# Two attentions of a decoder trunk: normalising after the product with the values

## The chip, the cores and the metric

The kernel runs on one core of one Trainium2 chip. The metric is the device time of one execution in microseconds, as the median of three runs; one further execution was recorded by the hardware profiler, and all rows shown here are from it. TensorE does the matrix products (PE in the rows; its weight loads are PEld and run beside the products), VectorE is DVE, ScalarE is ACT, GpSimd is POOL, SyncE (SP) issues the DMAs.

## The reference, cut to what matters

One layer of a trunk over 1024 positions of width 1024. Three branches (a latent attention, a forgetting attention, a state-space layer) are fed from one projection, gated, projected and summed; a gated feed-forward part with a convolution follows. Both attentions have 4 heads and this form:

```python
for i in range(seq // 128):                      # 8 query tiles
    s = q[tile i] @ k[:tile i + 1].T * scale     # (+ forget bias in one of them)
    p = softmax(where(causal, s, -1e30))
    out[tile i] = p @ v[:tile i + 1]             # values are 64 wide
```

All products keep float32 accuracy: each operand is split into a high part (fp32r) and the rest (lo), and three, or with exact weights two, products are added.

## The kernel before

The program is a chain of stages, each a block of five engine programs written out by hand with semaphores, and a barrier of all engines between blocks. The stage of the forgetting attention (names `fox_`, operands 66 wide) ends at 353 us of the span, that of the latent attention (`mla_`, `mlaa_`, 96 wide) at 576 us. Both end in a loop of the same class `Attention`, the first from 217 us on: 32 steps s = 0..31, step s is head h = s // 8 and query tile i = s % 8, with (i+1) x 128 keys. In between TensorE is given products of another part, the gates' projection (`GateFill`, L540), in fixed portions per step (`ATT_FILL`, `ATT_AHEAD`), so that it has work while the other engines deal with the softmax; the fill's matrix products need none of the attention's results.

One step goes through the engines so:

- TensorE `score` (L692, mask added by L694): scores into PSUM banks 0 to 3, two steps ahead of their use.
- VectorE `maximum` (L849): the row maximum. ScalarE `exponent` (L791): exponentials into `p_buf[s % 2]` and, by the accumulator, their row sum.
- VectorE `norm`: reciprocal of the sum (L855) and the whole row of exponentials times it, in place (L857).
- TensorE `turn` (L673; for queries and keys of the next head L678): 128 x 128 transposes through the identity, up to four into one PSUM bank. Each such bankful is a "fill of a bank", numbered in the list `fills`; fill f uses bank 4 + f % 2.
- ScalarE `split_hi` (L781) and VectorE `split_lo` (L862) empty the bank into the high and low parts of `pt`. Fill f of TensorE waits until fill f - 2 is emptied: `pe.wait_ge(self.lo, f - 1)`, since they share a bank. The semaphore `lo` counts VectorE's part.
- TensorE `values` (L720), every second step: the values times the turned rows of two query tiles, into bank 6. Four tiles (a group g, 8 in all) fill that bank. One half of its partitions has the product with the high part of the values, the other with the low part.
- ScalarE `out_low` (L805) copies the one half to `osum`, VectorE `out_sum` (L868) adds the other; for odd heads `out_hi` (L811) and `out_lo` (L875) split the sum for the next stage.

VectorE's order in step s is: `norm(s)`, with i = 7 the maximum of s + 1, `split_lo` of the fills of step s - 1, the maximum of s + 2 (not with i = 6), `split_lo` of the query and key fills, then `out_sum` (s % 4 = 1) or `out_lo` (s % 4 = 2). Engines run their programs strictly in order. TensorE's order at i = 5, where two bank fills of exponentials, p(s, first) and p(s, last), stand apart: first, six fill products, last; then step i = 6 begins with four fill products (`ATT_AHEAD`), the keys' fill, and so on.

After the last step TensorE does `values`, then `EDGE` = 10 fill products that cover the tail of the other engines, and the block ends with the barrier.

Of the kernel before, what the change touches and what calls it, by code (L numbers as in the profile page):

```python
# [21 lines left out]
P = 128  # L22
# [602 lines left out]
class Attention:  # L625
# [6 lines left out]

    def __init__(self, m, tag, kd, q_of, k_of, vv, q_t, k_t, p_buf, pt, osum, branch, ready, fill):
        self.m, self.kd, self.q_of, self.k_of, self.vv, self.q_t, self.k_t = m, kd, q_of, k_of, vv, q_t, k_t
        self.p_buf, self.pt, self.osum, self.branch, self.ready, self.fill = p_buf, pt, osum, branch, ready, fill
        (self.scores, self.negmax, self.exped, self.recip, self.normed, self.turned, self.hi, self.lo, self.pv,
         self.o_low, self.o_sum, self.o_hi, self.o_lo) = (m.sem(f"{tag}_{n}") for n in (
             "scores", "negmax", "exp", "recip", "norm", "turned", "hi", "lo", "pv", "o_low", "o_sum", "o_hi", "o_lo"))  # L640
        self.nmax, self.rsum, self.rinv = m.stat[:, 0:2], m.stat[:, 2:4], m.stat[:, 4:6]
        self.S = [m.ps[:, 2 * i:2 * i + 2, :].rearrange("p b n -> p (b n)") for i in range(2)]

        fills = [(w, 0, half) for w in "qk" for half in range(2)]
        for s in range(ATT_STEPS):
            fills += self.turned_in(s)
            fills += [("p", s, a, min(4, s % TT + 1 - a)) for a in range(0, s % TT + 1, 4)]
        self.fills = fills
        self.upto = {f[:2]: n + 1 for n, f in enumerate(fills)}
        self.at = {f: n for n, f in enumerate(fills)}  # L650

# [13 lines left out]
    def turn(self, pe, f):  # L665
        nc, m, x = self.m.nc, self.m, self.fills[f]
        if f >= 2:
            pe.wait_ge(self.lo, f - 1)
        bank = m.ps[:, 4 + f % 2, :]
        if x[0] == "p":  # L670
            _, s, a, n = x
            for j in range(n):
                tr = nc.tensor.transpose(bank[:, j * P:(j + 1) * P], self.p_buf[s % 2][:, (a + j) * P:(a + j + 1) * P], m.ident[:])  # L673
        else:
            what, h, half = x
            src = self.q_of if what == "q" else self.k_of
            for j in range(4):
                tr = nc.tensor.transpose(bank[0:self.kd, j * P:(j + 1) * P], src(h, 4 * half + j), m.ident[:])  # L678
        tr.then_inc(self.turned, 1)
# [44 lines left out]
    def tensor(self, pe):  # L724
        self.ready(pe)
        for what, n in zip("qk", OPENING):
            for f in self.fills_of(what, 0):
                self.turn(pe, f)
            self.fill.tensor(pe, n)
        self.score(pe, 0)  # L730
        self.score(pe, 1)
        for s in range(ATT_STEPS):
            i = s % TT
            if i == 7 and s + 1 < ATT_STEPS:
                self.score(pe, s + 1)
            if s + 2 < ATT_STEPS and i != 6:
                self.score(pe, s + 2)
            self.fill.tensor(pe, ATT_AHEAD[i])
            for f in self.qk_fills(s):
                self.turn(pe, f)  # L740
            pe.wait_ge(self.normed, s + 1)
            *first, last = self.fills_of("p", s)
            for f in first:
                self.turn(pe, f)

            if first:
                self.fill.tensor(pe, ATT_FILL[i])
            self.turn(pe, last)
            if not first:
                self.fill.tensor(pe, ATT_FILL[i])  # L750
            if s >= 2 and s % 2 == 0:
                self.values(pe, s // 2 - 1)
        self.values(pe, ATT_STEPS // 2 - 1)
        self.fill.tensor(pe, EDGE)


# [50 lines left out]
    def out_hi(self, act, g):  # L807
        h, half, _, _ = self.out_rows(g)
        if h % 2:
            act.wait_ge(self.o_sum, g + 1)  # L810
            self.m.nc.scalar.activation(self.m.br_hi[:, 2 * self.branch + h // 2, half * BANK:(half + 1) * BANK], self.osum[half],  # L811
                                        ACT.Copy).then_inc(self.o_hi, 1)

    def scalar(self, act):
        for what in "qk":
            for f in self.fills_of(what, 0):
                self.split_hi(act, f)
        self.exponent(act, 0)
        for s in range(ATT_STEPS):
            i = s % TT  # L820
            if s + 1 < ATT_STEPS:
                self.exponent(act, s + 1)
            if s % 4 == 1 and s > 4:
                self.out_low(act, s // 4 - 1)
            if s % 4 == 2 and s > 4:
                self.out_hi(act, s // 4 - 1)
            self.fill.scalar(act, ATT_AHEAD[i])
            for f in self.qk_fills(s):
                self.split_hi(act, f)
            *first, last = self.fills_of("p", s)  # L830
            for f in first:
                self.split_hi(act, f)
            if first:
                self.fill.scalar(act, ATT_FILL[i])
                self.fill.copy_made(act)
            self.split_hi(act, last)
            if not first:
                self.fill.scalar(act, ATT_FILL[i])
        g = ATT_STEPS // 4 - 1
        self.out_low(act, g)  # L840
        self.out_hi(act, g)
# [6 lines left out]
            dve.wait_ge(self.exped, s - 1)  # L848
        self.m.nc.vector.tensor_reduce(self.nmax[:, b:b + 1], self.S[b][:, 0:keys], AX.X, ALU.max, negate=True).then_inc(self.negmax, 1)  # L849

    def norm(self, dve, s):
        keys, b = (s % TT + 1) * P, s % 2
        V = self.m.nc.vector
        dve.wait_ge(self.exped, s + 1)
        V.reciprocal(self.rinv[:, b:b + 1], self.rsum[:, b:b + 1]).then_inc(self.recip, 1)  # L855
        dve.wait_ge(self.recip, s + 1)
        V.tensor_scalar(self.p_buf[b][:, 0:keys], self.p_buf[b][:, 0:keys], self.rinv[:, b:b + 1], None, ALU.mult).then_inc(self.normed, 1)  # L857

    def split_lo(self, dve, f):
        (hi, lo), src = self.place(f)  # L860
        dve.wait_ge(self.hi, f + 1)
        self.m.nc.vector.tensor_tensor(lo, src, f32(hi), ALU.subtract).then_inc(self.lo, 1)  # L862

    def out_sum(self, dve, g):
        h, half, main, _ = self.out_rows(g)
# [11 lines left out]
    def vector(self, dve):  # L877
# [5 lines left out]
        for s in range(ATT_STEPS + 1):  # L883
            h, i = divmod(s, TT)
            last = h + 1 >= H
            if s < ATT_STEPS:
                self.norm(dve, s)
            if i == 7 and not last:
                self.maximum(dve, s + 1)
            if s:  # L890
                for f in self.fills_of("p", s - 1):
                    self.split_lo(dve, f)
            if s + 2 < ATT_STEPS and i != 6:
                self.maximum(dve, s + 2)
            if s < ATT_STEPS:
# [1 line left out]
                    self.split_lo(dve, f)  # L897
            if s % 4 == 1 and s > 4:
                self.out_sum(dve, s // 4 - 1)
            if s % 4 == 2 and s > 4:  # L900
                self.out_lo(dve, s // 4 - 1)
        g = ATT_STEPS // 4 - 1
        self.out_sum(dve, g)
        self.out_lo(dve, g)


# [1955 lines left out]
```

## Time and profile before

| | |
|---|---|
| median of 3 runs | 1511.03 us (1509.42 to 1513.41) |
| profiled execution, its own time | 1511.12 us |
| its span in the profile | 1509.1 us |
| TensorE busy (products) | 1451.5 us, 96% of the span |
| VectorE busy | 1002.0 us, 66% |
| ScalarE busy | 652.2 us, 43% |
| TensorE idle in the forgetting attention, 216 to 353.2 us | 7.6 us in 12 waits |
| granted clock of TensorE, mean | 0.994 |

How to read the rows further down: in a timeline row stand the start in us, the duration in us (of all that are merged, where x is over 1), the engine, the line, the operation, what is written <- what is read, the shapes and the count; in square brackets the idle time of that engine just before and what ended it. In a row of waits stand who waited for whom, the total in us, how many times, and the longest.

### The profile page before, as it was taken

Reading aid. Unit: us, or ns where it says so; the run is one execution under the profiler, and the core shown is the slowest. Engines: PE = TensorE matmul, PEld = TensorE weight load, DVE = VectorE, ACT = ScalarE, POOL = GpSimd, SP = SyncE. Lnnn points to the kernel's source line nnn. Section 1 sums busy time; section 2 is a strip of 40 time slices with the busy share of each in tenths; the row PEclk is TensorE's granted clock in tenths of the full one; section 3 lists DMA queues with packets and bytes.
Section 4 is the critical chain, followed back from the end, with each engine's and each line's share of the span. In section 5 each row is a group of like instructions: output and inputs, shape, how many; then the busy total and the mean of one; then the engine's idle time right before and its main releaser. Section 6 shows DMA issues by size and latency. Waiting matters only on the chain.

```text
span 1509.1 us, 19008 instructions
## 1 busy us (share of the span) xinstructions
PE 1451.5 (96%) x7138; PEld 1218.5 (81%) x7138; DVE 1002.0 (66%) x1378; ACT 652.2 (43%) x1054; POOL 124.4 (8%) x104
## 2 busy tenths in 40 slices
PE   7999999998989998998999999999999999999999
PEld 6999887776877776886778888888888888888887
DVE  5211356665676666774872778877777787679786
ACT  6230235554435553124551255555555555444332
POOL 1000131001420003110210000000000000000000
PEclk9999999999999999999999999999999999999999
DMA  7101131113031102224664213222222221892222
GB/s 257 61 0 74 45 108 39 37 31 138 29 86 45 36 28 75 82 70 159 212 231 143 84 50 99 89 84 84 83 81 81 81 81 43 303 387 92 84 78 77
DMA packets 129941, 148.93 MB, mean 99 GB/s; under 512 B 11002, under 2 KB 94893, under 8 KB 129581
## 3 DMA queue, kind: packets, MB, share of 16 engines
q1 hardware_dynamic: 129664, 147.67, 29.6%
q8 instruction: 56, 0.92, 0.2%
q14 instruction: 32, 0.26, 0.1%
q10 hardware_dynamic: 189, 0.08, 0.0%
HBM read 110.83 MB, written 36.31 MB: 98 GB/s over the span
## 4 chain that ended last, share of the span: by engine, by line
PE 48%; issue 2%; DVE 1%; POOL 1%; ACT 0%; DMA 0%; POOLq 0%; DVEq 0%; ACTq 0%; SPq 0%
PE ps L1868 28%; PE ps L2175 4%; PE ps L2176 4%; PE ps L2177 4%; PE ps L2750 2%; PE ps L2751 2%; PE ps L2752 2%; POOL split_arena L2253 1%; PE ps L2264 1%; PE ps L2782 0%; DVE plain_arena L2271 0%; DMA plain_arena<-in_w_branch 0%; DVE plain_arena L2548 0%; PE ps L2760 0%; DVE down_all L2146 0%
## 5 line engine op out<-in xcount | busy, mean ns | idle before, releaser
L1868 PE MATMUL ps<-split_arena 128*128 128x512 f32 x1320 | 306.8, 389 | 0.0
L540 PE MATMUL ps<-split_arena 128*128 128x512 f32 x1152 | 290.0, 401 | 6.9 <-POOL split_arena L586 3.5
L1868 PEld LDWEIGHTS ps<-split_arena 128*128 128x128 f32 x1320 | 247.5, 188 | 51.5 <-issue 0.3
L540 PEld LDWEIGHTS ps<-split_arena 128*128 128x128 f32 x1152 | 211.1, 190 | 49.3 <-issue 5.7
L2051 ACT ACTIVATE down_ops<-down_all 128x1024 fp32r<-128x1024 f32 x77 | 81.6, 1061 | 115.5 <-PE ps L2177 112.1
L1868 PE MATMUL ps<-up_b,split_arena 128*128 128x512 f32 x528 | 126.5, 389 | 0.0
L2070 DVE TENSOR_TENSOR down_ops<-down_all,down_ops 128x1024 fp32r<-128x1024 f32 x77 | 94.1, 1223 | 46.3 <-ACT down_ops L2051 46.1
L2175 PE MATMUL ps<-down_ops 128*128 128x512 f32 x308 | 119.9, 389 | 0.5 <-DVE down_ops L2070 0.5
L2177 PE MATMUL ps<-down_ops 128*128 128x512 f32 x308 | 119.8, 389 | 0.0
L2176 PE MATMUL ps<-down_ops 128*128 128x512 f32 x308 | 119.8, 389 | 0.0
L1868 PEld LDWEIGHTS ps<-up_b,split_arena 128*128 128x128 f32 x528 | 99.1, 188 | 20.5
L327 PE MATMUL ps<-split_arena 128*128 128x426 f32 (+1 forms) x256 | 92.7, 362 | 2.2 <-DVE split_arena L213 2.2
L328 PE MATMUL ps<-split_arena 128*128 128x426 f32 (+1 forms) x256 | 91.5, 358 | 0.0
L329 PE MATMUL ps<-split_arena 128*128 128x426 f32 (+1 forms) x256 | 91.3, 357 | 0.0
L586 POOL TENSOR_TENSOR split_arena<-plain_arena,split_arena 128x1024 fp32r<-128x1024 f32 x23 | 61.0, 2652 | 347.6 <-ACT split_arena L564 347.6
L849 DVE TENSOR_REDUCE stat<-ps 128x1 f32<-128x128 f32 (+3 forms) x64 | 48.3, 755 | 51.9 <-PE ps L694 51.9
L465 DVE COPY plain_arena<-ps 128x426 f32<-128x426 f32 (+6 forms) x28 | 10.3, 406 | 104.0 <-PE ps L329 104.0
L2264 PE MATMUL ps<-split_arena 128*128 128x512 f32 x288 | 69.8, 401 | 6.4 <-PEq L2278 3.0
L575 ACT ACTIVATE plain_arena<-ps 128x512 f32<-128x512 f32 x48 | 28.6, 596 | 106.2 <-PE ps L540 61.5
L1796 DVE TENSOR_TENSOR split_arena<-up_s,split_arena 128x512 fp32r<-128x512 f32 x88 | 60.4, 687 | 18.3 <-ACT split_arena L1741 18.2
L2264 PEld LDWEIGHTS ps<-split_arena 128*128 128x128 f32 x288 | 54.6, 192 | 21.4 <-issue 5.6
L2175 PEld LDWEIGHTS ps<-down_ops 128*128 128x128 f32 x308 | 57.8, 188 | 13.0 <-DVE down_ops L2070 0.9
(359 smaller groups left out, 2523.6 us busy)
## 6 DMA issues: line engine op xcount, KB each, us to landing
plain_arena<-in_w_in SPq DMA_DIRECT2D x24, 512.0 KB, 4.1
scr_gate<-plain_arena SPq DMA_DIRECT2D x48, 256.0 KB, 2.0
plain_arena<-scr_gate SPq DMA_DIRECT2D x24, 512.0 KB, 4.3
plain_arena<-in_w_up SPq DMA_DIRECT2D x22, 512.0 KB, 5.3
up_raw<-in_w_up SPq DMA_DIRECT2D x22, 512.0 KB, 4.7
scr_act<-plain_arena SPq DMA_DIRECT2D x22, 512.0 KB, 2.7
down_all<-scr_act SPq DMA_DIRECT2D x18, 512.0 KB, 9.4
down_all<-in_w_down SPq DMA_DIRECT2D x18, 512.0 KB, 9.9
```

Source lines behind the costliest of these rows:

```text
L327: nc.tensor.matmul(o, hi, wh, start=(k == 0), stop=False)
L328: nc.tensor.matmul(o, hi, wl, start=False, stop=False)
L329: mm = nc.tensor.matmul(o, lo, wh, start=False, stop=(k == KD - 1))
L540: mm = nc.tensor.matmul(m.ps[:, self.banks[half], :], w[:, k, :], src[:, k, h * BANK:(h + 1) * BANK], start=(j == 0), stop=(j == self.PER_ ...
L586: self.m.nc.gpsimd.tensor_tensor(self.w_lo[u % 2], self.raw, f32(self.w_hi[u % 2]), ALU.subtract).then_inc(self.lo, 1)
L1868: mm = nc.tensor.matmul(o, self.w[j][w][:, k, :], self.h[j][k][h], start=(j in self.OPENS and k == 0 and n == 0), stop=(k == self.HK - 1 a ...
L2051: self.m.nc.scalar.activation(self.hi_of[n % 3], self.pair(n)[0], ACT.Copy).then_inc(self.hi, 1)
L2070: self.m.nc.vector.tensor_tensor(self.lo_of[n % 3], self.pair(n)[0], f32(self.hi_of[n % 3]), ALU.subtract).then_inc(self.lo, 1)
L2175: nc.tensor.matmul(o, a_hi[:, cut], b_hi, start=(k == 0 and j in self.OPENS), stop=False, skip_group_check=True)
L2176: nc.tensor.matmul(o, a_hi[:, cut], b_lo, start=False, stop=False, skip_group_check=True)
L2177: mm = nc.tensor.matmul(o, a_lo[:, cut], b_hi, start=False, stop=(k == HF - 1), skip_group_check=True)
L2264: mm = nc.tensor.matmul(proj_ps[u % 2][:, cut], w[:, k, :], src[:, 2 * n + k, cut], start=(k == 0 and w is hi and src is m.br_hi), stop=(k ...
```

## The change

The exponentials are turned and multiplied with the values as they are. VectorE takes only the reciprocal of each row sum (kept for 8 steps, `rinv` has 8 columns now), and the multiplication of the rows (L857) is left out. Instead the sums of four query tiles are scaled together: after the values of group g TensorE turns four columns of reciprocals, each read as a 128 x 128 tile by a stride of zero, into a bank as a new fill ("r", g), so that the bank holds the reciprocal of each query in all partitions; VectorE multiplies `osum` by it (`out_norm`). These fills stand in the same list and use the same two banks and the same semaphore `lo`. `out_hi` and `out_lo` come one step later than before.

```diff
         for s in range(ATT_STEPS):
             fills += self.turned_in(s)
             fills += [("p", s, a, min(4, s % TT + 1 - a)) for a in range(0, s % TT + 1, 4)]
+            if s % 4 == 1 and s > 4:
+                fills.append(("r", s // 4 - 1))
+        fills.append(("r", ATT_STEPS // 4 - 1))
...
         if f >= 2:
             pe.wait_ge(self.lo, f - 1)
         bank = m.ps[:, 4 + f % 2, :]
-        if x[0] == "p":
+        if x[0] == "r":
+            pe.wait_ge(self.recip, 4 * x[1] + 4)
+            for j in range(4):
+                row = 4 * (x[1] % 2) + j
+                tr = nc.tensor.transpose(bank[:, j * P:(j + 1) * P], self.rinv[:, row:row + 1].to_broadcast([P, P]), m.ident[:])
+        elif x[0] == "p":
...
-            pe.wait_ge(self.normed, s + 1)
+            pe.wait_ge(self.exped, s + 1)
...
             if s >= 2 and s % 2 == 0:
                 self.values(pe, s // 2 - 1)
+            if s % 4 == 1 and s > 4:
+                self.turn(pe, self.at["r", s // 4 - 1])
         self.values(pe, ATT_STEPS // 2 - 1)
+        self.turn(pe, self.at["r", ATT_STEPS // 4 - 1])
         self.fill.tensor(pe, EDGE)
...
         if h % 2:
-            act.wait_ge(self.o_sum, g + 1)
+            act.wait_ge(self.lo, self.at["r", g] + 1)
...
-            if s % 4 == 2 and s > 4:
+            if s % 4 == 3 and s > 4:
                 self.out_hi(act, s // 4 - 1)
...
-    def norm(self, dve, s):
-        keys, b = (s % TT + 1) * P, s % 2
-        V = self.m.nc.vector
+    def reciprocal(self, dve, s):
         dve.wait_ge(self.exped, s + 1)
-        V.reciprocal(self.rinv[:, b:b + 1], self.rsum[:, b:b + 1]).then_inc(self.recip, 1)
-        dve.wait_ge(self.recip, s + 1)
-        V.tensor_scalar(self.p_buf[b][:, 0:keys], self.p_buf[b][:, 0:keys], self.rinv[:, b:b + 1], None, ALU.mult).then_inc(self.normed, 1)
+
+        if s >= TT:
+            dve.wait_ge(self.turned, self.upto["r", s // 4 - 2])
+        self.m.nc.vector.reciprocal(self.rinv[:, s % TT:s % TT + 1], self.rsum[:, s % 2:s % 2 + 1]).then_inc(self.recip, 1)
...
+    def out_norm(self, dve, g):
+
+        h, half, main, _ = self.out_rows(g)
+        o, f = self.osum[half][main, :], self.at["r", g]
+        dve.wait_ge(self.o_sum, g + 1)
+        dve.wait_ge(self.turned, f + 1)
+        self.m.nc.vector.tensor_tensor(o, self.m.ps[main, 4 + f % 2, :], o, ALU.mult).then_inc(self.lo, 1)
...
-                self.norm(dve, s)
+                self.reciprocal(dve, s)
...
+            if s % 4 == 2 and s > 4:
+                self.out_norm(dve, s // 4 - 1)
...
-            if s % 4 == 2 and s > 4:
+            if s % 4 == 3 and s > 4:
                 self.out_lo(dve, s // 4 - 1)
         g = ATT_STEPS // 4 - 1
         self.out_sum(dve, g)
+        self.out_norm(dve, g)
         self.out_lo(dve, g)
```

TensorE's row at the end of step 5 and the start of step 6 of the forgetting attention (i = 5 to 6; L678 turns the keys, L673 the exponentials, L540 is the fill work), before:

```order
L673 MATMUL ps<-ident,plain_arena 128x128 [waits fox_lo,fox_norm]
L673 MATMUL ps<-ident,plain_arena 128x128 x3
L540 MATMUL ps<-split_arena 128x512 x6
L673 MATMUL ps<-ident,plain_arena 128x128 [waits fox_lo]
L673 MATMUL ps<-ident,plain_arena 128x128
L540 MATMUL ps<-split_arena 128x512 x4
L678 MATMUL ps<-ident,plain_arena 66x128 [waits fox_lo]
```

and with the change (L685 is the old L673, L690 the old L678, L681 the new transposes of reciprocals):

```order
L685 MATMUL ps<-ident,plain_arena 128x128 [waits fox_lo,fox_exp]
L685 MATMUL ps<-ident,plain_arena 128x128 x3
L540 MATMUL ps<-split_arena 128x512 x6
L685 MATMUL ps<-ident,plain_arena 128x128 [waits fox_lo]
L685 MATMUL ps<-ident,plain_arena 128x128
L681 MATMUL ps<-ident,stat 128x128 [waits fox_recip,fox_lo]
L681 MATMUL ps<-ident,stat 128x128 x3
L540 MATMUL ps<-split_arena 128x512 x4
L690 MATMUL ps<-ident,plain_arena 66x128 [waits fox_lo]
```

Between the last transposes of step 5 and the four fill products stand four transposes with a wait for `lo`; the wait of the first exponentials is for ScalarE's exponentials now and not for VectorE's scaling.

VectorE's row around the same place, from the query split of step 5 to the key split of step 6 (L868 is `out_sum`, L855 and L857 are `norm`, L862 is `split_lo`), before:

```order
L868 TENSOR_TENSOR plain_arena<-ps,plain_arena 64x512 [waits fox_o_low]
L855 RECIPROCAL stat<-stat 128x1 [waits fox_exp]
L857 TENSOR_SCALAR plain_arena<-plain_arena,stat 128x896 [waits fox_recip]
L862 TENSOR_TENSOR fox_pt_1386<-ps,fox_pt_1385 128x4x128 [waits fox_hi]
L862 TENSOR_TENSOR fox_pt_1386<-ps,fox_pt_1385 128x2x128 [waits fox_hi]
L862 TENSOR_TENSOR split_arena<-ps,split_arena 66x512 [waits fox_hi]
```

and with the change, one head later (L890 is `out_sum`, L871 the reciprocal, L876 `split_lo`, L884 `out_norm`):

```order
L890 TENSOR_TENSOR plain_arena<-ps,plain_arena 64x512 [waits fox_o_low]
L871 RECIPROCAL stat<-stat 128x1 [waits fox_turned,fox_exp]
L876 TENSOR_TENSOR fox_pt_1386<-ps,fox_pt_1385 128x4x128 [waits fox_hi]
L876 TENSOR_TENSOR fox_pt_1386<-ps,fox_pt_1385 128x2x128 [waits fox_hi]
```

The scaling is gone between the reciprocal and the two splits; behind them `out_norm` (L884, 64x512, waits fox_turned and fox_o_sum) is queued, ahead of the keys' split.

## Rows read from the trace of the kernel before

**Rows 1.** Page, part 1: busy time, share of the span, instructions.
```profile
PE 1451.5 (96%) x7138; PEld 1218.5 (81%) x7138; DVE 1002.0 (66%) x1378; ACT 652.2 (43%) x1054; POOL 124.4 (8%) x104
```
**Rows 2.** Windows of both attentions: length, busy PE, PEld, DVE, ACT, POOL, clock, DMA.
```profile
216.00:355.00 139.00, 130.66 (x800) 107.75 (x799) 85.98 (x174) 72.60 (x155) 10.36 (x22) 1.00 0.13 40
...
437.00:578.00 141.00, 130.93 (x793) 108.08 (x794) 85.81 (x174) 73.58 (x155) 11.30 (x7) 0.99 0.12 35
```
**Rows 3.** Waits of TensorE, forgetting attention, 216 to 353.2 us.
```profile
PE ps L678 <- DVE fox_pt L862: 1.9, 3, 0.9
PE ps L673 <- DVE plain_arena L857: 1.7, 3, 0.6
PE ps L720 <- DVE fox_pt L862: 1.5, 1, 1.5
PE ps L673 <- DVE split_arena L862: 1.2, 3, 0.4
```
**Rows 4.** The same, latent attention, 436 to 576.2 us.
```profile
PE ps L678 <- DVE mla_pt L862: 1.9, 3, 0.9
```
**Rows 5.** Groups on VectorE, forgetting attention: busy us, mean ns, idle before.
```profile
L857 DVE TENSOR_SCALAR plain_arena<-plain_arena,stat 128x128 f32<-128x128 f32 (+7 forms) x32 | 17.9, 558 | 1.1
...
L868 DVE TENSOR_TENSOR plain_arena<-ps,plain_arena 64x512 f32<-64x512 f32 x8 | 5.5, 686 | 5.8 <-ACT plain_arena L805 5.8
```
**Rows 6.** Timeline, head 1, end of i = 5 and i = 6.
```profile
275.96 1.17 PE L540 MATMUL ps<-split_arena 128*128 128x512 f32 x4
...
276.34 0.16 DVE L855 RECIPROCAL stat<-stat 128x1 f32<-128x1 f32 x1
...
276.54 0.69 DVE L857 TENSOR_SCALAR plain_arena<-plain_arena,stat 128x896 f32<-128x896 f32 x1
277.26 1.02 DVE L862 TENSOR_TENSOR fox_pt<-ps,fox_pt 128x512 fp32r<-128x512 f32 x2
...
278.01 0.63 PE L678 MATMUL ps<-ident,plain_arena 128*66 128x128 f32 x4 [0.88 <-DVE fox_pt L862]
...
278.47 0.60 PE L673 MATMUL ps<-ident,plain_arena 128*128 128x128 f32 x4
...
278.83 1.17 PE L540 MATMUL ps<-split_arena 128*128 128x512 f32 x4
```
**Rows 7.** Timeline, the same place in heads 0, 2 and 3.
```profile
245.60 0.63 PE L678 MATMUL ps<-ident,plain_arena 128*66 128x128 f32 x4 [0.48 <-DVE fox_pt L862]
...
310.02 0.62 PE L678 MATMUL ps<-ident,plain_arena 128*66 128x128 f32 x4 [0.50 <-DVE fox_pt L862]
...
341.50 0.63 PE L673 MATMUL ps<-ident,plain_arena 128*128 128x128 f32 x4 [0.78 <-DVE fox_pt L862]
```
**Rows 8.** Timeline, head 1, i = 2 (step 10).
```profile
259.92 1.14 PE L692 MATMUL ps<-split_arena 66*128 66x512 f32 x6
...
260.79 0.14 DVE L855 RECIPROCAL stat<-stat 128x1 f32<-128x1 f32 x1
...
260.91 0.23 PE L694 MATMUL ps<-maskb,identb 128*128 128x128 bf16 x1
...
261.57 0.41 DVE L862 TENSOR_TENSOR fox_pt<-ps,fox_pt 128x256 fp32r<-128x256 f32 x1
...
261.71 0.55 PE L673 MATMUL ps<-ident,plain_arena 128*128 128x128 f32 x3 [0.57 <-DVE plain_arena L857]
```
**Rows 9.** Timeline, from head 1 to head 2 (steps 15 and 16).
```profile
285.62 0.68 DVE L862 TENSOR_TENSOR fox_pt<-ps,fox_pt 128x512 fp32r<-128x512 f32 x1
...
286.46 0.29 PE L673 MATMUL ps<-ident,plain_arena 128*128 128x128 f32 x1
```
**Rows 10.** Timeline, end of the forgetting attention and the barrier.
```profile
350.87 0.69 DVE L868 TENSOR_TENSOR plain_arena<-ps,plain_arena 64x512 f32<-64x512 f32 x1 [2.82 <-ACT plain_arena L805]
...
352.26 0.69 DVE L875 TENSOR_TENSOR split_arena<-plain_arena,split_arena 128x512 fp32r<-128x512 f32 x1 [0.70 <-ACT split_arena L811]
...
353.27 8.90 PE L540 MATMUL ps<-split_arena 128*128 128x512 f32 x38 [0.71 <-PEq L941]
```

More of the change, by code:

```diff
@@ L637, in __init__ @@
         self.p_buf, self.pt, self.osum, self.branch, self.ready, self.fill = p_buf, pt, osum, branch, ready, fill
-        (self.scores, self.negmax, self.exped, self.recip, self.normed, self.turned, self.hi, self.lo, self.pv,
+        (self.scores, self.negmax, self.exped, self.recip, self.turned, self.hi, self.lo, self.pv,
          self.o_low, self.o_sum, self.o_hi, self.o_lo) = (m.sem(f"{tag}_{n}") for n in (
-             "scores", "negmax", "exp", "recip", "norm", "turned", "hi", "lo", "pv", "o_low", "o_sum", "o_hi", "o_lo"))
-        self.nmax, self.rsum, self.rinv = m.stat[:, 0:2], m.stat[:, 2:4], m.stat[:, 4:6]
+             "scores", "negmax", "exp", "recip", "turned", "hi", "lo", "pv", "o_low", "o_sum", "o_hi", "o_lo"))
+        self.nmax, self.rsum, self.rinv = m.stat[:, 0:2], m.stat[:, 2:4], m.stat[:, 4:12]
         self.S = [m.ps[:, 2 * i:2 * i + 2, :].rearrange("p b n -> p (b n)") for i in range(2)]
@@ L647, in __init__ @@
             fills += [("p", s, a, min(4, s % TT + 1 - a)) for a in range(0, s % TT + 1, 4)]
+            if s % 4 == 1 and s > 4:
+                fills.append(("r", s // 4 - 1))
+        fills.append(("r", ATT_STEPS // 4 - 1))
         self.fills = fills
+        self.hi_upto = [sum(x[0] != "r" for x in fills[:f + 1]) for f in range(len(fills))]
         self.upto = {f[:2]: n + 1 for n, f in enumerate(fills)}
@@ L849, in maximum @@
         self.m.nc.vector.tensor_reduce(self.nmax[:, b:b + 1], self.S[b][:, 0:keys], AX.X, ALU.max, negate=True).then_inc(self.negmax, 1)
-    def norm(self, dve, s):
-        keys, b = (s % TT + 1) * P, s % 2
-        V = self.m.nc.vector
+    def reciprocal(self, dve, s):
         dve.wait_ge(self.exped, s + 1)
-        V.reciprocal(self.rinv[:, b:b + 1], self.rsum[:, b:b + 1]).then_inc(self.recip, 1)
-        dve.wait_ge(self.recip, s + 1)
-        V.tensor_scalar(self.p_buf[b][:, 0:keys], self.p_buf[b][:, 0:keys], self.rinv[:, b:b + 1], None, ALU.mult).then_inc(self.normed, 1)
+        if s >= TT:
+            dve.wait_ge(self.turned, self.upto["r", s // 4 - 2])
+        self.m.nc.vector.reciprocal(self.rinv[:, s % TT:s % TT + 1], self.rsum[:, s % 2:s % 2 + 1]).then_inc(self.recip, 1)
     def split_lo(self, dve, f):
         (hi, lo), src = self.place(f)
-        dve.wait_ge(self.hi, f + 1)
+        dve.wait_ge(self.hi, self.hi_upto[f])
         self.m.nc.vector.tensor_tensor(lo, src, f32(hi), ALU.subtract).then_inc(self.lo, 1)
+    def out_norm(self, dve, g):
[4 more added lines that the diff above has]
+        self.m.nc.vector.tensor_tensor(o, self.m.ps[main, 4 + f % 2, :], o, ALU.mult).then_inc(self.lo, 1)
     def out_sum(self, dve, g):
```

## The prediction

> **What bounds the kernel now.** I read the page first: TensorE is busy for 96% of the span and VectorE for two thirds [rows 1]. So an instruction on TensorE costs its full time, and one taken off VectorE is worth only what TensorE waits for it. Then the windows of the two attentions, which are the only stretches that change: TensorE is busy for 130.7 of 139 us and 130.9 of 141 us, VectorE for 86 [rows 2]. Then TensorE's waits there. In the forgetting attention they are: the keys' fill at i = 6 for a bank that VectorE must empty (1.9 us in 3), the exponentials of i = 2 for the scaling itself (1.7 us in 3), the last values (1.5 us), and the second fill at i = 7 (1.2 us in 3) [rows 3]. The latent attention has the same 1.9 us in 3 at the keys' fill [rows 4]; the two loops run alike, so I work out one and double it. The scaling is 17.9 us of VectorE in 32 pieces, but only those small waits of TensorE hang on it [rows 3, 5]. Last, I read the timeline at the places where the new fill stands.
>
> **The change part by part.** Per attention: 32 scalings go from VectorE (17.9 us), 8 multiplications of 64 x 512 come, of the kind of `out_sum`, 0.69 us each, 5.5 us in all [rows 5]. VectorE gains 12.4 us of slack, which is worth nothing in itself. TensorE gets 8 fills of 4 transposes, after i = 1 of heads 1 to 3 (3 times), after i = 5 of all heads (4 times), and at the end (once).
>
> *Price of one such fill.* The trace shows no transpose of a column read with stride zero. The nearest rows are the keys' transposes, 0.46 us from their start to that of the next, and the exponentials', 0.36 us [rows 6]. I take 0.40 us. Below, 0.36 us is the end: four passes through the array cannot be free on an engine that does nothing beside them. Above, the four 128 x 512 products of the same rows with 1.17 us are the end.
> The Trainium skill (TensorE: Matmul & The Clock Gate, section LDWEIGHTS) has the load of a stationary operand depend on its columns alone, about 107 ns for 128 columns, whatever stands in them; four would be an estimated 0.43 us, and the sum would be higher by some 0.4 us than with my value. No run here shows it for a column of stride zero.
>
> *After i = 5, 4 times.* TensorE's program now has, behind the last transposes of the step and ahead of the four `ATT_AHEAD` products, the fill "r". Fill f waits for fill f - 2, and f - 2 is the first fill of the same step's exponentials. VectorE empties it only in step 6, behind `out_sum` and the reciprocal. So a wait that stood behind the four products comes to stand in front of them. In head 1: TensorE is ready at 275.96 us. The scaling (276.54, 0.69 us) is gone, so the split moves from 277.26 to 276.54. TensorE started 0.75 us after the start of that split (278.01 against 277.26), so "r" starts at 277.29, after 1.33 us of idle time. It takes 0.40. The four products then take 1.0 (1.17 with the end of the last, which overlaps the next by about 0.2, as 278.47 + 0.60 against 278.83 shows). The keys' fill starts at 278.69 where it started at 278.01 [rows 6]: 0.68 us later. What it needs, the split of p(13, last), is ready at about 277.7. The next in the same bank as "r", the exponentials of i = 6, needs `out_norm`: turned at 277.9, multiplied by 278.6, asked for at 279.1. That fits with 0.5 us. Behind it VectorE has only the keys' split, which waits for the keys' fill and ScalarE anyway. In heads 0, 2 and 3 the same fill waits 0.48, 0.50 and 0.78 us at this place [rows 7], and each loses the same cover of four products; I take +0.7 for each. 4 x 0.7 = 2.8 us.
>
> *After i = 1, 3 times.* Here "r" follows six fill products, and its f - 2 is long emptied, so it does not wait. Then the exponentials of i = 2 (three transposes, 261.71) waited 0.57 us for the scaling, which ends this wait [rows 8]. What is late next is the bank: the inserted fill shifts the parity, so they now need the split of p(9), one fill back. It follows the reciprocal (260.79 + 0.14) and takes 0.41, so ends at 261.38, and TensorE can start at 261.43. On TensorE's own side, without waiting they would start 0.07 behind the mask (260.91), at 260.98, plus 0.40 for "r": 261.38. So 261.43 against 261.71: -0.28 each, -0.84 us in all. The scaling's wait is gone, but the new transposes fill most of it. `out_norm` then delays the maximum of i = 4 by about 0.2 us; its exponentials are asked for two steps later, so this is hidden.
>
> *Step 16, once.* `out_lo` of group 2 moves from step 14 to the end of step 15, behind the last keys' split. VectorE's split of p(15, first) started at 285.62, partly beside the scaling of step 16 (0.2 us of delay, which goes). With 0.69 us ahead of it, it starts at 286.13 and ends at 286.8; the exponentials of step 16 share its bank and started at 286.46 [rows 9]. +0.4 us. The other three `out_lo` fall where VectorE has been waiting for TensorE. `out_hi` goes into ScalarE's idle time at i = 7, which is longer than its 0.63 us by a little; I take nothing for it, and up to 0.2 if that is not so.
>
> *The end, once.* The chain values, `out_low`, `out_sum`, `out_hi`, `out_lo` ends later than the ten `EDGE` products: TensorE waits 0.71 us at the barrier [rows 10]. `out_norm` comes into this chain with 0.69 and a semaphore, +0.7 us. The "r" fill ahead of `EDGE` delays TensorE by 0.4, which lies inside the barrier's wait, so it costs nothing here. The wait for the last values (1.5 us) is the time from the last transposes through ScalarE and VectorE's splits, with no scaling in it; it stays.
>
> *Sum.* 2.8 - 0.84 + 0.4 + 0.7 = 3.06 us per attention, 6.1 us for both. The profiled execution took 1511.12 us, its span 1509.1; it stands 0.1 us off the median of 1511.03, so I correct nothing: 1511.12 + 6.1 = 1517.2 us. The likeliest case has its own range: with 0.36 us for a fill, and nothing for step 16 and the end, 2.7 - 0.84 = 1.9 per attention, 1514.9; with 0.5 us for a fill and 0.9 at each i = 5, about 1519.5.
>
> **The rivals.**
> *Dear transposes.* If a stationary operand with stride zero loads slowly, and a fill costs the 1.17 us of the upper end, each i = 5 loses 0.77 more and each i = 2 turns from -0.28 to +0.44 (260.98 + 1.17 = 262.15): 4 x 1.47 + 3 x 0.44 + 0.4 + 0.7 = 8.3 us per attention, 1527.7 us. For it: no row shows the access. Against it: both kinds of transposes in the rows cost alike, whatever they read.
> *The wait only changes its place.* If VectorE, freed, comes to the split at i = 6 so much earlier that the keys' fill starts when it did, the four places cost nothing: -0.84 + 0.4 + 0.7 = 0.3 per attention, 1511.7 us. It decides from about 0.7 us of lead. For it: 12.4 us of slack per attention. Against it: VectorE waits for TensorE's scores in every head just ahead of this place, so its lead is set back there, and only the one scaling of 0.69 us lies between.
> *Faster.* VectorE's queue was what made TensorE wait at i = 2, 6 and 7 (1.7 + 1.9 + 1.2 = 4.8 us per attention [rows 3]); with the scalings gone, all these waits vanish and the new transposes fit into them. With +0.7 at the end that is -4.1 per attention, 1502.9 us. It decides where the split of the first exponentials of i = 5 is done by the time TensorE is through with that step: 1.3 us earlier than I have it. For it: half of these waits follow a scaling directly. Against it: at i = 7 the chain is keys' fill, ScalarE, VectorE, with no scaling in it, and eight new fills are 3.2 us of TensorE's time.
>
> **How the numbers follow.** The sum as worked out 0.66, dear transposes 0.08, the changed place 0.19, faster 0.07. What this kernel's measurement can tell from no change is about 0.3%, 4.5 us, so slower begins at 1515.6. Of the likeliest case a tenth lies below that. Slower: 0.60 + 0.08 = 0.68; same: 0.19 + 0.06 = 0.25; faster: 0.07. The range from 1511.3 to 1520.5 us holds the sum with its bounds and the changed place, and leaves out the faster case and the dear one. The likeliest case alone is 1514.9 to 1519.5.
>
> **What would show each step.** In the new profile: TensorE's new transposes after i = 5 stand behind an idle time of 1.1 to 1.4 us ended by VectorE's split, 8 times in both attentions, and no wait is left at the keys' fill of i = 6. The first-to-next distance of the new fill is 0.36 to 0.46 us. The exponentials of i = 2 wait less than 0.1 us, and for a split. The first exponentials of head 2 wait about 0.4 us. The barrier wait of TensorE stays at about 1 us (0.7 + 0.7 - 0.4). VectorE's busy time falls by about 25 us and the span does not follow. I am wrong if the time falls, if the new transposes at i = 5 do not wait, or if some cost lies outside the two attentions.

## The result, and the profile after

The changed kernel takes 1515.65 us (median of 9 runs, 1514.56 to 1519.24), the kernel before beside it 1511.83 us: a ratio of 1.0031, 95% interval 1.0021 to 1.0042, so 3 to 6 us slower. In a second series of runs it was 1.0035 (1.0022 to 1.0048). 1517.2 us was forecast, inside a range from 1511.3 to 1520.5. The profiled execution took 1519.24 us and is the longest of the nine; its span is 1517.5 us, 8.4 more than that of before. Not all of this is the change, as the stretches show.

The page's engine totals (answer to [rows 1]):

```profile
PE 1461.9 (96%) x7202; PEld 1227.6 (81%) x7202; DVE 978.5 (64%) x1330; ACT 652.5 (43%) x1054; POOL 125.8 (8%) x104
```

VectorE is busy 23.5 us less, TensorE 10.4 us more. The waits of TensorE from 216 us to the barrier behind the forgetting attention (answer to [rows 3]; who waited for whom, total, times, longest):

```profile
PE ps L681 <- DVE fox_pt L876: 3.3, 4, 1.1
PE ps L732 <- DVE fox_pt L876: 1.5, 1, 1.5
PE ps L685 <- DVE split_arena L876: 1.2, 3, 0.4
PE ps L704 <- ACT plain_arena L806: 0.5, 1, 0.5
```

The waits of the keys' fill and of the scaled exponentials are gone. In their place stands one of the new transposes (L681) for VectorE's split (L876), 3.3 us in 4 (0.68, 1.07, 0.68 and 0.90 us in heads 0 to 3). All waits together are 6.5 us where they were 7.6, and the attention is longer all the same: eight fills of transposes have come. The place behind i = 5 of head 1 in the timeline (answer to [rows 6]; the columns are start, duration, engine, line):

```profile
277.46 0.38 PE L685 MATMUL ps<-ident,plain_arena 128*128 128x128 f32 x2
...
277.97 0.16 DVE L871 RECIPROCAL stat<-stat 128x1 f32<-128x1 f32 x1
...
278.16 1.02 DVE L876 TENSOR_TENSOR fox_pt<-ps,fox_pt 128x512 fp32r<-128x512 f32 x2
...
278.91 0.65 PE L681 MATMUL ps<-ident,stat 128*128 128x128 f32 x4 [1.07 <-DVE fox_pt L876]
...
279.32 1.18 PE L540 MATMUL ps<-split_arena 128*128 128x512 f32 x4
279.67 0.69 DVE L884 TENSOR_TENSOR plain_arena<-ps,plain_arena 64x512 f32<-64x512 f32 x1 [0.48 <-PE ps L681]
...
280.33 0.60 PE L690 MATMUL ps<-ident,plain_arena 128*66 128x128 f32 x4
...
280.77 0.60 PE L685 MATMUL ps<-ident,plain_arena 128*128 128x128 f32 x4
```

TensorE is through with step 13 at about 277.6. VectorE's reciprocal and split follow each other with no scaling between. The new transposes start 0.75 us after the start of the split, idle for 1.07 us before, and only then come the four covering products. The keys' fill starts at 280.33. At i = 2 (answer to [rows 8]):

```profile
262.21 1.23 PE L704 MATMUL ps<-split_arena 66*128 66x512 f32 x6
...
262.73 0.15 DVE L871 RECIPROCAL stat<-stat 128x1 f32<-128x1 f32 x1
262.80 0.40 DVE L876 TENSOR_TENSOR fox_pt<-ps,fox_pt 128x256 fp32r<-128x256 f32 x1
...
263.12 0.67 DVE L884 TENSOR_TENSOR plain_arena<-ps,plain_arena 64x512 f32<-64x512 f32 x1
...
263.29 0.23 PE L706 MATMUL ps<-maskb,identb 128*128 128x128 bf16 x1
...
263.35 0.51 PE L685 MATMUL ps<-ident,plain_arena 128*128 128x128 f32 x3
```

The split of p(9) ends at 263.20, and the exponentials (263.35) follow the mask (263.29) with no wait. In head 2 it is not so:

```profile
295.12 0.69 DVE L890 TENSOR_TENSOR plain_arena<-ps,plain_arena 64x512 f32<-64x512 f32 x1 [0.98 <-ACT plain_arena L820]
...
295.85 0.16 DVE L871 RECIPROCAL stat<-stat 128x1 f32<-128x1 f32 x1
...
296.04 0.42 DVE L876 TENSOR_TENSOR fox_pt<-ps,fox_pt 128x256 fp32r<-128x256 f32 x1
...
296.29 0.23 PE L706 MATMUL ps<-maskb,identb 128*128 128x128 bf16 x1
...
296.62 0.52 PE L685 MATMUL ps<-ident,plain_arena 128*128 128x128 f32 x3
```

The split ends at 296.46, behind the mask's start, and the exponentials start 0.33 us behind the mask. Step 16 (answer to [rows 9]) and the end of the attention (answer to [rows 10]):

```profile
287.53 0.68 DVE L897 TENSOR_TENSOR split_arena<-plain_arena,split_arena 128x512 fp32r<-128x512 f32 x1
...
288.12 0.15 DVE L871 RECIPROCAL stat<-stat 128x1 f32<-128x1 f32 x1
288.20 1.48 DVE L876 TENSOR_TENSOR fox_pt<-ps,fox_pt 128x512 fp32r<-128x512 f32 x2
...
288.69 0.23 PE L706 MATMUL ps<-maskb,identb 128*128 128x128 bf16 x1
...
289.01 0.30 PE L685 MATMUL ps<-ident,plain_arena 128*128 128x128 f32 x1
```

```profile
354.20 0.69 DVE L890 TENSOR_TENSOR plain_arena<-ps,plain_arena 64x512 f32<-64x512 f32 x1 [2.83 <-ACT plain_arena L820]
354.93 0.69 DVE L884 TENSOR_TENSOR plain_arena<-ps,plain_arena 64x512 f32<-64x512 f32 x1
355.66 0.63 ACT L826 ACTIVATE split_arena<-plain_arena 128x512 fp32r<-128x512 f32 x1 [1.49 <-DVE plain_arena L884]
356.33 0.69 DVE L897 TENSOR_TENSOR split_arena<-plain_arena,split_arena 128x512 fp32r<-128x512 f32 x1 [0.70 <-ACT split_arena L826]
...
357.34 8.90 PE L540 MATMUL ps<-split_arena 128*128 128x512 f32 x38 [1.02 <-PEq L966]
```

In the first, `out_lo` (L897) stands ahead of the reciprocal, and the exponentials of step 16 start at 289.01, 0.32 us behind the mask. In the second, the multiplication (L884, 354.93) has come into the chain, and TensorE waits 1.02 us at the barrier where it waited 0.71.

To find where the time of one attention went, I took the start of the same instruction in both traces and followed how the difference grows. The forgetting attention starts at 217.40 us before and at 218.77 us after. These 1.37 us have come up ahead of anything that is changed.

| place (forgetting attention) | before | after | the difference grows by |
|---|---|---|---|
| first query transposes | 217.40 | 218.77 | (1.37 at the start) |
| keys' fill at i = 6, head 0 | 245.60 | 247.66 | +0.69 |
| i = 7, head 0, to i = 2, head 1 | 261.71 | 263.35 | -0.42 (of it -0.31 at i = 2) |
| keys' fill at i = 6, head 1 | 278.01 | 280.33 | +0.68 |
| exponentials of step 16 | 286.46 | 289.01 | +0.23 (+0.26 at the place) |
| exponentials at i = 2, head 2 | 294.10 | 296.62 | -0.03 |
| keys' fill at i = 6, head 2 | 310.02 | 313.22 | +0.68 |
| exponentials at i = 2, head 3 | 326.13 | 328.93 | -0.40 (of it -0.28 at i = 2) |
| exponentials at i = 6, head 3 | 341.50 | 344.87 | +0.57 |
| barrier | 353.27 | 357.34 | +0.70 (+0.74 from the last values on) |
| sum from 217.40 on | | | +2.70 |

The latent attention from its first transposes to the barrier went from 138.82 us (437.45 to 576.27) to 141.51 us (440.43 to 581.94): +2.69. So the two attentions hold 5.4 us of the 8.4. The other 3 us are in places that the change doesn't touch: the 1.37 at the front, and 2.9 in the state-space stage (576.27 to 708.45 us before, 581.94 to 717.02 after), less 1.1 that TensorE waits less for a DMA between the attentions and 0.2 behind the state-space stage. The granted clock differs there. Windows of the kernel before (length, busy PE, PEld, DVE, ACT, POOL, clock, DMA share, GB/s):

```profile
580.00:720.00 140.00, 127.09 (x670) 104.11 (x671) 93.86 (x124) 41.65 (x63) 23.41 (x15) 0.96 0.35 106
```

and of the changed kernel over the same stretch:

```profile
580.00:720.00 140.00, 125.56 (x657) 101.39 (x657) 89.24 (x122) 37.62 (x57) 26.62 (x15) 0.94 0.30 92
```

It is 0.96 before and 0.94 after, from 580 to 720 us.

### The profile page after: what moved, and what is told of

Its sections match the earlier page's. It is cut to its first block, busy times and chain, and to the rows that moved or that the text cites. A ratio compares the mean times of both kernels' runs of the same rounds, so it can differ in the third digit from the quotient of the medians.

```text
span 1517.5 us, 19166 instructions
## 1 busy us (share of the span) xinstructions
PE 1461.9 (96%) x7202; PEld 1227.6 (81%) x7202; DVE 978.5 (64%) x1330; ACT 652.5 (43%) x1054; POOL 125.8 (8%) x104
## 4 chain that ended last, share of the span: by engine, by line
PE 48%; DVE 2%; issue 1%; ACT 1%; DVEq 0%; POOL 0%; ACTq 0%
PE ps L1893 28%; PE ps L2200 4%; PE ps L2202 4%; PE ps L2201 4%; PE ps L2776 2%; PE ps L2777 2%; PE ps L2775 2%; DVE plain_arena L2296 1%; PE ps L2289 1%; PE ps L2807 0%; DVE plain_arena L2573 0%; ACT plain_arena L2272 0%; DVE split_arena L2578 0%; PE ps L2785 0%; DVE split_arena L2583 0%
## 5 line engine op out<-in xcount | busy, mean ns | idle before, releaser
L540 PE MATMUL ps<-split_arena 128*128 128x512 f32 x1152 | 291.8, 402 | 8.2 <-POOL split_arena L586 3.5
L540 PEld LDWEIGHTS ps<-split_arena 128*128 128x128 f32 x1152 | 212.0, 191 | 51.3 <-issue 7.3
## 6 DMA issues: line engine op xcount, KB each, us to landing
down_all<-in_w_down SPq DMA_DIRECT2D x18, 512.0 KB, 10.4
```

The costliest lines, as they stand in the source:

```text
L540: mm = nc.tensor.matmul(m.ps[:, self.banks[half], :], w[:, k, :], src[:, k, h * BANK:(h + 1) * BANK], start=(j == 0), stop=(j == self.PER_ ...
```

## Experiments

In all comparisons "attention" is the forgetting attention, from the start of its first transposes to the first product behind its barrier, on TensorE, in the profiled execution. Before: 135.87 us; changed: 138.57 us.

**1. The changed kernel once more.** No edit.

> The changed kernel once more, beside the others of this call. Theory (queue order: the new fill waits for the bank in front of the four covering products): the loss lies in the two attentions alone, 2.7 and 2.8 us from their first transposes to the barrier behind them, 5.5 us in all; with what the runs scatter the time is 1514.5 to 1518 us. The 3 us that the first trace shows more in the state-space stage (from 580 to 708 us) are scatter and will not come again. Rival (the change also costs something behind the attentions): the state-space stage is again 3 us longer than in the kernel before.

Measured: 1517.14 us against 1511.15, 1.0035 (1.0022 to 1.0048). The attention is 138.58 us (219.28 to 357.86). The state-space stage took 131.06 us (584.39 to 715.45) where the first trace of the same kernel has 135.08 and the kernel before 132.18, so the 3 us did not come again, and the rival is out. One more profiled execution of the kernel before was to show the other half of this:

> One more look at the kernel before, to see how far the stretches outside the attentions scatter from one execution to the next: 1509 to 1515 us; the attentions' own lengths the same within 0.1 us, the state-space stage (576 to 700 us) different by up to 3 us if its length is scatter.

Measured: 1511.84 us, span 1509.8; the attention is 135.90 us (217.83 to 353.73). So the attention repeats to 0.03 us, and its 2.7 us are real. The kernel before hardly scattered in its two traces: its latent attention is 138.82 and 138.78 us, its state-space stage 132.18 and 132.04, where up to 3 us had been allowed for. The changed kernel did: 4.0 us in the state-space stage, at a clock of 0.94 and 0.98 from 580 to 720 us, and this time the latent attention was 1.5 us longer (143.03), while nothing of it but its opening differs: from the query transposes of i = 3 of head 0 on it is 123.0 us as in the first trace. The clock in the opening was 0.87 in this trace,

```profile
445.00:460.00 15.00, 13.29 (x67) 10.89 (x66) 5.58 (x14) 8.08 (x18) 2.37 (x1) 0.87 0.08 24
```

where the first trace of the same kernel had 0.99:

```profile
445.00:460.00 15.00, 13.29 (x79) 11.15 (x78) 6.42 (x15) 8.37 (x19) 2.40 (x1) 0.99 0.08 24
```

Ahead of this window the clock was alike, 0.90 and 0.89 from 430 to 445 us. The 1.5 us lie between the exponentials of i = 0 and those of i = 2 in head 0: six products of the fill work take 2.10 us to the next group's start there (451.62 to 453.72), where they took 1.47 (450.72 to 452.19). So a difference of 3 us between two spans of this kernel says nothing.

**2. The fill behind the covering products.** The turn of reciprocals goes from the end of step i = 5 (and 1) to step i = 6 (and 2).

```diff
             self.fill.tensor(pe, ATT_AHEAD[i])
+            if s % 4 == 2 and s > 4:
+                self.turn(pe, self.at["r", s // 4 - 1])
             for f in self.qk_fills(s):
...
-            if s % 4 == 1 and s > 4:
-                self.turn(pe, self.at["r", s // 4 - 1])
```

> The fill of reciprocals is turned in the next step, behind the four covering products, and not in front of them. Theory (the stall of 1.1 to 1.3 us in front of the covering products is the loss): at i = 6 the keys' fill starts 0.3 us earlier than in the kernel before, then the exponentials wait up to 0.5 us for the multiplication to empty the bank, and the next wait of 0.47 us goes; the four places cost about nothing instead of 0.7 each. Per attention -0.66 at i = 2, +0.26 at step 16, +0.74 at the end: +0.3, so 1511 to 1513 us, about 4.5 us less than the changed kernel. Rival (the transposes' own 0.4 us and the multiplications are the loss, wherever they stand): within 1 us of the changed kernel.

Measured: 1510.4 us against 1511.15, ratio 0.9993 (0.9985 to 1.0002), with the same instructions; this is a little below the 1511 to 1513 that were expected. The attention is 136.26 us (218.66 to 354.92), 2.3 us less than the changed kernel's and 0.4 more than before, where 0.3 was expected. The rival is out. TensorE's and VectorE's rows at i = 6 of head 1:

```profile
277.02 1.17 PE L540 MATMUL ps<-split_arena 128*128 128x512 f32 x4
...
277.60 1.02 DVE L876 TENSOR_TENSOR fox_pt<-ps,fox_pt 128x512 fp32r<-128x512 f32 x2
...
278.35 0.65 PE L681 MATMUL ps<-ident,stat 128*128 128x128 f32 x4 [0.16 <-DVE fox_pt L876]
...
278.83 0.60 PE L690 MATMUL ps<-ident,plain_arena 128*66 128x128 f32 x4
279.11 0.69 DVE L884 TENSOR_TENSOR plain_arena<-ps,plain_arena 64x512 f32<-64x512 f32 x1 [0.48 <-PE ps L681]
...
279.94 0.63 PE L685 MATMUL ps<-ident,plain_arena 128*128 128x128 f32 x4 [0.51 <-DVE plain_arena L884]
...
280.33 0.94 PE L540 MATMUL ps<-split_arena 128*128 128x512 f32 x3
```

The new transposes wait 0.16 us and no more, for the four products now run while VectorE gets there. The price is the next wait: the exponentials (L685) need the same bank and wait 0.51 us for the multiplication (L884). So 2.3 of the 2.7 us that the changed kernel loses in an attention are the order of four transposes and four products.

**3. The removed part alone.**

```diff
-            pe.wait_ge(self.normed, s + 1)
+            pe.wait_ge(self.exped, s + 1)
...
-        dve.wait_ge(self.recip, s + 1)
-        V.tensor_scalar(self.p_buf[b][:, 0:keys], self.p_buf[b][:, 0:keys], self.rinv[:, b:b + 1], None, ALU.mult).then_inc(self.normed, 1)
```

> The kernel before with the scaling of the rows left out and nothing in its place: the outputs of the attentions are not normalised. It prices the removed part alone. Theory (only TensorE's waits behind a scaling go): the keys' fill at i = 6 gets 0.48, 0.68, 0.50 and 0.7 us earlier, the exponentials of i = 2 0.57 us three times: -4.0 us per attention, -8 us, 1503 to 1505 us. Rival (VectorE is not on the path, the scaling was hidden): less than 2 us off the kernel before. Second rival (VectorE's queue makes all waits): -12 us or more.

Measured: 1502.51 us, ratio 0.9935 (0.9918 to 0.9953), 7 to 12 us less, and a little below the 1503 to 1505 that were expected. The attention is 130.79 us (218.82 to 349.61), 5.1 less, where I had 4.0. The scaling was worth more than the forecast gave it: the exponentials at i = 2 come 0.73 us earlier each, not 0.57, and the four places at i = 6 gain 0.64, 0.75, 0.65 and 0.72 us, 2.76 in all and not 2.36. In the trace they follow the mask without a wait:

```profile
261.47 0.14 DVE L855 RECIPROCAL stat<-stat 128x1 f32<-128x1 f32 x1
261.54 0.40 DVE L860 TENSOR_TENSOR fox_pt<-ps,fox_pt 128x256 fp32r<-128x256 f32 x1
...
261.59 0.23 PE L694 MATMUL ps<-maskb,identb 128*128 128x128 bf16 x1
...
261.66 0.50 PE L673 MATMUL ps<-ident,plain_arena 128*128 128x128 f32 x3
```

The row of before [rows 8] gives 0.57 us as idle. But between the start of the mask and that of the exponentials lay 0.80 us, and here it is 0.07. The idle time in a row counts from the end of the row ahead, and the mask's row is 0.23 us long; a product that needn't wait starts inside it. The missing 0.16 is this overlap, 0.23 less 0.07.

**4. Both, the scaling and the new fill.**

```diff
-            pe.wait_ge(self.exped, s + 1)
+            pe.wait_ge(self.normed, s + 1)
...
+        dve.wait_ge(self.recip, s + 1)
+        row = self.p_buf[s % 2][:, 0:(s % TT + 1) * P]
+        self.m.nc.vector.tensor_scalar(row, row, self.rinv[:, s % TT:s % TT + 1], None, ALU.mult).then_inc(self.normed, 1)
```

> The changed kernel with the scaling of the rows kept as well (the sums are then divided twice, so the attentions' outputs are too small). Theory (the new fill waits behind VectorE's queue): the scaling comes back into the chain in front of the new fill, 4 x 0.69, and of the exponentials of i = 2, 3 x 0.6, and 0.2 at step 16: +4.8 per attention, about +9.6 us against the changed kernel, 1523 to 1527 us. Rival (the scaling is hidden now that the exponentials are read unscaled anyway): under +3 us.

Measured: 1526.83 us against 1511.15, ratio 1.0097 (1.0082 to 1.0112), 9.7 us over the changed kernel. The attention is 144.01 us (218.24 to 362.25), +5.4 against the 4.8 of the theory. TensorE's waits in it:

```profile
PE ps L681 <- DVE fox_pt L879: 6.2, 4, 1.8
PE ps L685 <- DVE fox_pt L879: 2.2, 4, 0.7
```

The new transposes wait 6.2 us where they waited 3.3: 0.7 more at each of the four places, the length of one scaling; and the exponentials (L685) wait 2.2 us in 4, where the changed kernel's rows of waits have none for these splits. What stands ahead of the split on VectorE sets the start of these transposes one for one.

**5. A place without a wait.** The fill for the first half of a head is turned in the next head behind the six products of i = 0, that of the last head ahead of the last values; 16 columns of reciprocals.

```diff
-            if s % 4 == 1 and s > 4:
+            if s % TT == 1 and s > 4:
                 fills.append(("r", s // 4 - 1))
-        fills.append(("r", ATT_STEPS // 4 - 1))
+            if s % TT == 0 and s:
+                fills.append(("r", s // 4 - 2))
+        fills += [("r", ATT_STEPS // 4 - 2), ("r", ATT_STEPS // 4 - 1)]
...
```

The rest of the edit moves the transposes, the multiplication and the two splits of each group to the steps that follow from this.

> As the changed kernel, but the fill of reciprocals for the first half of a head (which stood behind i = 5) is turned in the next head, behind the six products of i = 0, for the last head in the 1.5 us that TensorE waits ahead of the last values. Reciprocals have 16 columns for it. Theory: at i = 5 and 6 nothing of the change is left but the missing scaling, so the keys' fill is 0.48 to 0.68 us earlier than in the kernel before (-2.3 per attention), the three fills at i = 0 cost their own 0.36 (+1.1), i = 2 gives -0.66, the end +0.74: -1.1 per attention, about 2.3 us under the kernel before and 7.6 under the changed one, 1508 to 1510 us. Rival (VectorE's multiplications behind the splits of i = 0 and 1 delay the exponentials there): no faster than the kernel before.

Measured: 1509.53 us against 1511.53, ratio 0.9984 (0.9973 to 0.9996). The attention is 134.62 us (217.44 to 352.06), 1.25 less than before, where 1.1 was expected; its terms are less close. The four places at i = 6 gain 2.6 us and not 2.3, and each of the three fills at i = 0 costs 0.56 and not 0.36. At i = 0 the new transposes (L683 here) follow the products at once and cost 0.36 us until the values (L734) start:

```profile
285.42 1.64 PE L540 MATMUL ps<-split_arena 128*128 128x512 f32 x6
...
286.90 0.60 PE L683 MATMUL ps<-ident,stat 128*128 128x128 f32 x4
...
287.26 2.08 PE L734 MATMUL ps<-fox_pt,split_arena 128*128 128x256 f32 x16
```

The next step adds to this: the fill shifts the parity, so the exponentials of i = 1 now need the split of i = 0 (289.75, 0.29 long) and come another 0.18 us later (in head 2 at 290.18, 0.25 behind the mask, where before it was 0.06). The rival's multiplication is not the cause, for it stands behind this split.

This version beats both kernels, by little: its interval against the kernel before ends at 0.9996.

**6. More cover at the barrier.** `EDGE` is 14 instead of 10, in the version of 5 and in the kernel before.

```diff
-EDGE = 10
+EDGE = 14
```

> The same with 14 instead of 10 products of the fill work behind the last values (EDGE), at every place that uses it. Theory: TensorE waits 1.0 us at each barrier behind an attention; four more products of 0.22 us cover 0.9 of it, twice: -1.8 us against r_late, 1506 to 1508 us. Rival: the products only move, and the next block starts with a wait for data that they hid: no difference to r_late.

> The kernel before with EDGE = 14. TensorE waits 0.7 us at each of the two barriers, of which 0.3 is the barrier's own latency: -0.8 to -1.4 us, 1509.8 to 1510.4. If r_late_edge14 gains by the barriers only as much as this one, the end term of the sum (+0.74 by the multiplication) is not covered by more products. Rival: no difference.

Measured: 1511.41 us, ratio 0.9991 (0.9981 to 1.0002), and 1513.56 us, ratio 1.0010 (0.9999 to 1.0021). Both forecasts missed. TensorE's wait at the barriers fell from 1.02 to 0.30 us in the one and from 0.71 to 0.30 in the other, and nothing was gained. The rival was right: the products only move. In the state-space stage TensorE has four products less to do before it waits for GpSimd, and waits for it longer by as much. With 14,

```profile
588.31 3.67 PE L1481 MATMUL ps<-ident,plain_arena 128*128 128x128 f32 x16 [4.07 <-POOL plain_arena L1423]
```

and with 10:

```profile
587.38 1.97 PE L1481 MATMUL ps<-ident,plain_arena 128*128 128x128 f32 x16 [3.12 <-POOL plain_arena L1423]
```

That is 4.07 us against 3.12, and these transposes start 12.73 us behind the barrier with 14 and 12.72 with 10 (barriers at 575.58 and 574.66). The forgetting attention itself is 0.15 us longer (134.77), in the kernel before 0.6 (136.51). The remaining difference between the medians of the two, about 1.9 us, is of the size of the scatter, and I leave it open.

**The latent attention as a second sample.** Its opening, from the first query transposes to those of i = 3 in head 0, took 18.4 to 18.5 us in five of the ten traces and 20.0 to 20.1 in the other five, and the changed kernel had it both ways, so this is not the change. Behind the opening, up to the barrier, the latent attention repeats and shows the same differences as the forgetting one:

| kernel | forgetting attention | latent, behind its opening |
|---|---|---|
| before, two traces | 135.87, 135.90 | 120.38, 120.35 |
| changed, two traces | 138.57, 138.58 | 122.99, 123.00 |
| 2, fill behind the products | 136.26 | 120.63 |
| 3, scaling left out | 130.79 | 115.20 |
| 4, scaling and new fill | 144.01 | 128.38 |
| 5, a place without a wait | 134.62 | 119.03 |

## Why the prediction was right

By its own steps, in us per attention:

| step | forecast | trace |
|---|---|---|
| new fill in front of the covering products, 4 times | +2.8 | +2.62 (0.69, 0.68, 0.68, 0.57) |
| scaling's wait replaced, i = 2, 3 times | -0.84 | -0.62 (-0.31, -0.03, -0.28) |
| `out_lo` ahead of step 16 | +0.4 | +0.26 |
| multiplication in the chain to the barrier | +0.7 | +0.74 |
| small shifts (0.03 to 0.04 behind each wait that has gone, 0.08 at steps 8 and 24) | not seen | -0.30 |
| sum | +3.06 | +2.70 |

Doubled, 6.1 us against 5.4. The measured ratio says 3 to 6.

- *The price of a fill.* 0.40 was taken, between 0.36 and 1.17. From the new transposes to what follows it is 0.35 us at i = 1 (294.87 to 295.22 in head 2), 0.36 in experiment 5, and 0.41 right behind a wait. The mask of i = 2, further down, comes 0.44 us later, so 0.40 was about right. A stationary operand of stride zero costs what a dense one costs: the load of one (L681) takes 0.136 us in the median, that of the exponentials (L685) 0.141. The dear case is out: its 1.17 would have shown in every one of these places. The Trainium skill (TensorE: Matmul & The Clock Gate, section LDWEIGHTS) makes the load depend on the columns alone, about 107 ns for 128; the trace agrees that the stride of zero costs nothing, and its 0.136 us for one load are somewhat above the page's figure. The prediction's argument that both kinds of transposes cost alike was loose: its rows have 0.46 and 0.36 us [rows 6].
- *The wait in front of the cover.* Forecast were 1.1 to 1.4 us of idle time ahead of the new transposes; the rows have 0.68, 1.07, 0.68 and 0.90. As above, the idle time in a row leaves out the overlap with the product ahead, so I had it 0.25 too high in head 1. In heads 0 and 2 it is 0.4 less again, as it was before the change (0.48 and 0.50 against 0.88, [rows 6, 7]), and the forecast range had left this out. The shift of the keys' fill doesn't hang on it. The start, 0.75 us behind the split's, and the shift of the keys' fill by 0.68 came out to the hundredth. That this order makes 2.3 of the 2.7 us is shown by experiment 2, and that the wait follows VectorE's queue by experiment 4.
- *i = 2.* In heads 1 and 3 the wait vanished, as forecast. In head 2 only 0.03 us were gained. There `out_sum` writes partitions 64 to 127, and the reciprocal behind it starts 0.73 us after it (295.12 to 295.85) and not 0.61 (262.12 to 262.73). The split behind the reciprocal is late by another 0.12 (0.19 us after it, 296.04, and not 0.07, 262.80). So the split that TensorE needs is 0.24 us later, and 0.33 us lie between mask and exponentials. The term was taken as the same for the three heads, and is not.
- *Step 16.* 0.26 and not 0.4: from the reciprocal to the split it was 0.38 us before (285.24 to 285.62) and is 0.08 now (288.12 to 288.20). The scaling between them gave 0.3 us back, and I had counted 0.2. Mechanism and place were right.
- *The rival with the changed place* (1511.7 us) needed a lead of VectorE of 0.7 us at the split; it had none, since the maximum of step 15 still waits for TensorE (2.43 us before it, 2.33 in the kernel before). *The faster case* fell by the same, and by i = 7, whose three waits of 0.4 us are the same in both traces.
- *VectorE's time:* 25 us less forecast, 23.5 measured, and the span did not follow.

The sum was 0.7 us too high; what the traces give, 5.4 us, lies in the measured 3 to 6. That the forecast of 1517.2 us is so near the 1517.14 of the second series is in part luck: the sum started from 1511.12 us, 0.7 below the nine-run median of 1511.83, and this offsets its being too high; the terms themselves were off by up to 0.3 us per attention, in both directions. What makes the clock go down in those stretches in one execution and not in another was not tried.

## What to carry to other kernels

Work that is taken off an engine with slack is worth only the waits that end on it; here 17.9 us of VectorE were worth 5.1 us per attention when nothing came in their place, and the replacement, 8 fills and 8 multiplications, cost 7.8 (the changed kernel's 2.7 and the 5.1). A new instruction that waits must be put behind the independent work of its queue, not in front: behind four products instead of in front of them the same transposes cost some 0.6 us less at each of four places. Where buffers alternate by a running number, an inserted element also changes who waits for whom behind it; list for each the element two back, and who empties it.

## What the runs showed that I had not expected

- A wait of TensorE costs more than the idle time in its row: 0.57 idle behind the mask, 0.73 us gained when it went. Without a wait the next product starts 0.07 us behind the mask's start, inside its row of 0.23.
- A VectorE instruction behind one that writes partitions 64 to 127 started 0.12 us later than behind the same on partitions 0 to 63 (0.73 against 0.61 us from start to start). The Trainium skill (VectorE: DVE Perf Modes, section Two Vector instructions with no wait between them) has such an instruction held until the earlier ones have finished, where its output or an input begins in another group of 32 partitions than that of the instruction ahead; these rows agree, for the held reciprocal starts behind the end of `out_sum` (295.85, end 295.81) and the other ahead of it (262.73, end 262.80).
- The same 0.12 us came up at three places in the kernel before. In head 1, where `out_sum` writes partitions 64 to 127, from query split to `out_sum`, from `out_sum` to reciprocal and from scaling to split pass 0.71, 0.72 and 0.72 us (from 274.91); in head 0 0.59, 0.60 and 0.60 (from 242.89). The keys' fill waits 0.88 us in head 1 and 0.48 in head 0.
- Like stretches of the program ran with another granted clock in two executions of the same (changed) kernel: 0.99 and 0.87 from 445 to 460 us, 0.94 and 0.98 from 580 to 720 us. With it went 1.5 us in the opening of the latent attention and 4.0 us in the state-space stage, next to 5.4 us of the change.
